# Down projection by seven products: weight sums prepared on GpSimd among the z products, low parts of two units in one operation

## The reference

```python
def layer(x, pos, lp, cache):
    a_u, a_v, b_q, b_k, b_v, c_q, c_k, c_v, c_o, c_logi, c_logf = project(
        x, pos, lp['attn_norm'], lp['w_in'], lp['gmlp_norm'], lp['mlstm_gate_b'])
...
    x = x + mixed @ lp['w_out']
    y, conv_state = conv_ffn(x, lp['ffn_norm'], lp['w_up'], lp['conv_w'], lp['conv_b'], lp['w_down'], conv_buf)
    x = x + y
...

def conv_ffn(x, g, w_up, conv_w, conv_b, w_down, conv_buf):
    up = rmsnorm(x, g) @ w_up
    T = up.shape[1]
    full = jnp.concatenate([conv_buf.astype(up.dtype), up], axis=1)
    c = conv_b + full[:, 0:T] * conv_w[0]
    for j in range(1, CONV_W):
        c = c + full[:, j:j + T] * conv_w[j]
    y = (jax.nn.gelu(c[..., :D_FF], approximate=False) * c[..., D_FF:]) @ w_down
    return y, full[:, -(CONV_W - 1):]
```

## Time and profile before

| | |
|---|---|
| runs (us) | 2410.37, 2413.76, 2416.2; median 2413.76 |
| profiled execution | 2414.81 us, of which the span of the trace is 2413.0 us |
| mean granted TensorE clock | 0.995 |
| busy: TensorE / VectorE / ScalarE / GpSimd | 98% / 70% / 46% / 31% of the span |
| DMA | 264.83 MB, mean 110 GB/s |

### The profile page before, as it was taken

One profiled execution on the slowest core, in us unless ns is written; L12 is line 12 of the kernel. 1 busy time (PEld: TensorE's weight loads), 2 busy tenths in 40 slices (PEclk: granted clock), 3 DMA queues, 4 the chain that ended last, 5 costly groups with the idle time before them and its releaser, 6 DMA issues.

```text
span 2413.0 us, 42532 instructions
## 1 busy us (share of the span) xinstructions
PE 2360.4 (98%) x16563; PEld 2315.0 (96%) x16563; DVE 1682.6 (70%) x2875; ACT 1116.8 (46%) x2227; POOL 742.7 (31%) x732
## 2 busy tenths in 40 slices
PE   9999999999999999999999999999999999998999
PEld 8999998999999998999999999999999999998999
DVE  3115687888788877888611256877987888779884
ACT  6325676544433433345523366655333333333563
POOL 0001254432222223664110013452322222245630
PEclk9999999999999999999999999999999999999999
DMA  4442432212221224454524334321222222253564
GB/s 155 135 142 89 147 114 53 73 64 81 72 80 64 81 72 150 161 165 137 196 73 139 120 125 136 100 60 54 81 78 74 72 73 75 86 214 93 161 198 148
DMA packets 248348, 264.83 MB, mean 110 GB/s; under 512 B 16822, under 2 KB 212564, under 8 KB 245972
## 3 DMA queue, kind: packets, MB, share of 16 engines
q1 hardware_dynamic: 248148, 262.11, 34.3%
HBM read 211.95 MB, written 50.11 MB: 109 GB/s over the span
## 4 chain that ended last, share of the span: by engine, by line
PE 78%; DVE 12%; issue 4%; POOL 2%; ACT 2%; DMA 2%; SPq 0%; DVEq 0%; POOLq 0%; ACTq 0%
PE bank L401 24%; PE bank L403 23%; PE bank L402 23%; DVE sA L2729 3%; DVE sB L2731 3%; PE bank L1367 1%; PE bank L1292 1%; PE bank L1337 1%; DMA grr<-g_scratch 1%; DVE xT L2740 1%; DVE tb L2726 1%; PE bank L1377 1%; POOL wN L2187 1%; POOL acc L453 1%; DVE sD L2731 1%
## 5 line engine op out<-in xcount | busy, mean ns | idle before, releaser
L401 PE MATMUL bank<-actH,wb 128*128 128x384 f32 (+1 forms) x1712 | 560.8, 328 | 1.5 <-DVE actL L2607 1.3
L402 PE MATMUL bank<-actL,wb 128*128 128x384 f32 (+1 forms) x1712 | 555.5, 324 | 0.0
L403 PE MATMUL bank<-actH,wb 128*128 128x384 f32 (+1 forms) x1712 | 555.1, 324 | 0.0
L401 PE MATMUL bank<-wzH,actH 128*128 128x256 f32 (+3 forms) x1296 | 369.4, 285 | 2.8 <-issue 1.5
L403 PE MATMUL bank<-wzH,actL 128*128 128x256 f32 (+3 forms) x1296 | 364.2, 281 | 0.0
L402 PE MATMUL bank<-wzL,actH 128*128 128x256 f32 (+3 forms) x1296 | 363.9, 281 | 0.0
L401 PEld LDWEIGHTS bank<-actH,wb 128*128 128x128 f32 x1712 | 322.8, 189 | 6.2 <-issue 3.2
L402 PEld LDWEIGHTS bank<-actL,wb 128*128 128x128 f32 x1712 | 323.7, 189 | 0.7
L403 PEld LDWEIGHTS bank<-actH,wb 128*128 128x128 f32 x1712 | 323.7, 189 | 0.0
L401 PEld LDWEIGHTS bank<-wzH,actH 128*128 128x128 f32 (+1 forms) x1296 | 236.3, 182 | 4.9 <-issue 2.0
L402 PEld LDWEIGHTS bank<-wzL,actH 128*128 128x128 f32 (+1 forms) x1296 | 236.5, 182 | 0.0
(11 more groups left out here) (361 smaller groups left out, 5526.6 us busy)
## 6 DMA issues: line engine op xcount, KB each, us to landing
raw<-in_w_up SPq DMA_DIRECT2D x88, 512.0 KB, 4.5
g_scratch<-cv SPq DMA_DIRECT2D x44, 545.0 KB, 3.1
rawz<-in_w_in SPq DMA_DIRECT2D x22, 1024.0 KB, 5.4
zb<-z_scratch SPq DMA_DIRECT2D x16, 1156.0 KB, 6.1
z_scratch<-zst SPq DMA_DIRECT2D x128, 128.0 KB, 1.8
raw<-in_w_out SPq DMA_DIRECT2D x128, 128.0 KB, 2.9
grr<-g_scratch SPq DMA_DIRECT2D x38, 384.0 KB, 3.3
raw<-in_w_down SPq DMA_DIRECT2D x50, 256.0 KB, 3.4
```

What stands on the lines that cost most here:

```text
L401: pe.matmul(out, aH, bH, start=first, stop=False, skip_group_check=goes_on)
L402: pe.matmul(out, aH, bL, start=False, stop=False, skip_group_check=goes_on)
L403: return pe.matmul(out, aL, bH, start=False, stop=last, skip_group_check=goes_on)
```

## The change

Weight sums. A DRAM scratch `ws_scratch` takes the four weight sums of each j. They are made among the z products: SyncE loads both row blocks of pair i (1 MB, `load_parts`) into one of two places of `stg` behind the store of unit 9 + 3i, GpSimd makes four sums of 512 columns (`weight_parts`), and SyncE stores them (1 MB, `store_sums`) behind the store of unit 13 + 3i, ahead of `next_wz` and `load_mixers` at the same u. `load_parts(i)` waits for the store of pair i − 2. `stg` lies where `zb0` lies, so `load_zb(0)` waits for the last two stores. GpSimd makes the sums of pairs 0 to 5 ahead of its `memset`s and those of 6 to 10 behind them.

Down products. `w_down` is no longer kept; `load_w` brings for each step the two weight operands, raw or summed. High parts (`step_high`) and low parts (`step_parts`) are made for both halves in one operation (1024 and 768 wide) for p < 3; p = 3 keeps 512 and 384. All gate sums, T2 among them, are GpSimd's (`gate_sum`, 44 per layer). The parts of steps 0 to 4 are made among the taps of the last up products; before, those of the first seven units. There are four operand slots, by t mod 4; gates stay in `pbA` and `pbB`. Both adds of product pair p − 1 follow step j = 1 of p. The `convst` transposes move behind unit (3, 1, 2) into bank 2, ScalarE's copy to p = 3, j = 6, the store behind the ninth load of the last chunk. The loads of the last chunk wait for later steps (`load_half(j)` for j < 4: steps 40 and 41; before: the first unit of p = 3).

```diff
+        ws_dram = nc.dram_tensor("ws_scratch", (DEPTH, NJ, P, 4, 512), F32, kind="Internal").ap()
...
+        def w_slot(t):
+            return sA0 if t % 4 == 0 else sA3 if t % 4 == 3 else sA1[:, t % 4 - 1]
+        def g_slot(t):
+            return sB3 if t % 4 == 3 else sB[:, t % 4]
+        def g_pair(j):
+            return pbA[:, j] if j < 6 else pbB[:, j - 6]
+        def w_parts(t):
+            if t < 3 * NJ:
+                return w_raw(t)[:, 0:2], w_slot(t)[:, 0:2, 0], w_slot(t)[:, 0:2, 1]
+            return w_raw(t)[:, 1], w_slot(t)[:, 1, 0], w_slot(t)[:, 1, 1]
+        def g_parts(t):
+            p, j = t // NJ, t % NJ
             if p == 3:
+                return g_pair(j)[:, 1], sD[:, j % 4, 0], sD[:, j % 4, 1]
+            src = grr[:, j % 3, 1:3] if p == 2 else g_pair(j)[:, 0:2]
+            return src, g_slot(t)[:, 0:2, 0], g_slot(t)[:, 0:2, 1]
...
+        def step_low(l, t):
+            return l * N_W + 2 * NF + 2 * t + 2
+        def slot_free(l, t):
+            if t < 4:
+                return tile_mm(l, NF - 1, (2, 6, 9, 9)[t])
+            p, j = (t - 4) // NJ, (t - 4) % NJ
+            if t >= 3 * NJ:
+                return unit_mm(l, p, 1, j)
+            return max(unit_mm(l, p, h, j) for h in range(2))
...
+                    elif i == 0:
+                        sp.wait_ge(ws_st[0], ws_stored(l, NJ - 1))
+                        sp.wait_ge(ws_st[1], ws_stored(l, NJ - 2))
...
+                def load_parts(i):
+                    if i >= 2:
+                        sp.wait_ge(ws_st[i % 2], ws_stored(l, i - 2))
+                    sp.dma_start(stg[:, i % 2, 0:4].rearrange("p (k h) n -> p k (h n)", k=2),
+                                 w_down[2 * i * P:2 * i * P + 2 * P, :].rearrange("(k p) n -> p k n", p=P)).then_inc(ws_in[i % 2], 16)
+                def store_sums(i):
+                    sp.wait_ge(s_r, w_sum_at(l, i, 3))
+                    sp.dma_start(ws_dram[l, i], stg[:, i % 2, 1:5]).then_inc(ws_st[i % 2], 16)
                 for u in range(Z1):
                     store_z(u)
+                    if u >= 9 and u % 3 == 0 and u // 3 - 3 < NJ:
+                        load_parts(u // 3 - 3)
+                    if u >= 13 and u % 3 == 1 and u // 3 - 4 < NJ:
+                        store_sums(u // 3 - 4)
                     if u == 5:
                         next_wz(2)
...
+                    if t >= 4:
+                        sp.wait_ge(w_l, step_low(l, t - 4))
+                    place, r0, r1 = w_raw(t), slice(2 * j * P, 2 * j * P + P), slice(2 * j * P + P, 2 * j * P + 2 * P)
                     if p == 0:
-                        sp.dma_start(w_raw(f), w_down[f * P:f * P + P, :]).then_inc(ld_in[t % 3], 16)
-                    c = slice(0, 512) if p == 1 else slice(512, 1024)
-                    sp.dma_start(w_raw(f + 1)[:, c], w_down[f * P + P:f * P + 2 * P, c]).then_inc(ld_in[t % 3], 16)
+                        sp.dma_start(place[:, 0], ws_dram[l, j, :, 3]).then_inc(ld_in[t % 3], 16)
+                        sp.dma_start(place[:, 1], w_down[r0, 0:512]).then_inc(ld_in[t % 3], 16)
+                    elif p == 1:
+                        sp.dma_start(place[:, 0:2], ws_dram[l, j, :, 1:3]).then_inc(ld_in[t % 3], 16)
+                    elif p == 2:
+                        sp.dma_start(place[:, 0], w_down[r1, 0:512]).then_inc(ld_in[t % 3], 16)
+                        sp.dma_start(place[:, 1], ws_dram[l, j, :, 0]).then_inc(ld_in[t % 3], 16)
+                    else:
+                        sp.dma_start(place[:, 1], w_down[r1, 512:1024]).then_inc(ld_in[t % 3], 16)
...
+                    if p in (1, 3):
+                        sp.wait_ge(w_l, step_low(l, t - NJ if p == 1 else t - 2 * NJ))
+                    elif p == 2 and j >= 3:
+                        sp.wait_ge(w_l, step_low(l, t - 3))
+                    pair = g_pair(j)
+                    if p == 0:
+                        sp.dma_start(pair.rearrange("p c t -> p (c t)"), g_dram[l, 2 * j, :, 0:768]).then_inc(ld_in[t % 3], 16)
+                    elif p == 1:
+                        sp.dma_start(pair[:, 1], g_dram[l, 2 * j + 1, :, 0:384]).then_inc(ld_in[t % 3], 16)
+                    elif p == 2:
+                        sp.dma_start(grr[:, j % 3, 0:2].rearrange("p c t -> p (c t)"), g_dram[l, 2 * j + 1, :, 0:768]).then_inc(ld_in[t % 3], 16)
+                        sp.dma_start(grr[:, j % 3, 2], g_dram[l, 2 * j, :, 0:384]).then_inc(ld_in[t % 3], 16)
+                    else:
+                        sp.dma_start(pair[:, 1], g_dram[l, 2 * j + 1, :, 384:768]).then_inc(ld_in[t % 3], 16)
...
+                load_w(2)
                 for t in range(3):
                     load_gs(t)
-                load_gs(3)
-                for t in range(2, 5):
+                for t in range(3, 4 * NJ):
                     load_w(t)
-                for t in range(4, 4 * NJ):
                     load_gs(t)
-                    if t + 1 < 3 * NJ:
-                        load_w(t + 1)
-                    if t == 7:
+                    if t == 9:
                         store_g(NF - 1)
-                    if t == 8:
-                        sp.wait_ge(gv_st, l * 16 + 16)
-                        sp.wait_ge(sto_r, 2 * l + 2)
-                        for s, dst in ((0, "prompt_conv"), (1, "sample_conv")):
-                            sp.dma_start(O[dst][l, 0].rearrange("r (a b) -> (r a) b", b=P), cvo[:, s]).then_inc(cvo_st, 16)
+                def store_conv():
+                    sp.wait_ge(gv_st, l * 16 + 16)
+                    sp.wait_ge(sto_r, 2 * l + 2)
+                    for s, dst in ((0, "prompt_conv"), (1, "sample_conv")):
+                        sp.dma_start(O[dst][l, 0].rearrange("r (a b) -> (r a) b", b=P), cvo[:, s]).then_inc(cvo_st, 16)
 
                 def load_half(j):
                     h, f, q = j // NF, j % NF, j % 4
                     if j < 4:
-                        sp.wait_ge(w_l, unit_low(l, 3, 1, 0))
+                        sp.wait_ge(w_l, step_low(l, 4 * NJ - 4 + j // 2))
...
+                        if j == 8:
+                            store_conv()
...
-                    if (p, h, j) == (0, 0, 0):
+                    if (p, h, j) == (3, 1, 2):
                         pe.wait_ge(cvs_r, (l + 1) * 4 * NF)
+                        pe.wait_ge(bank_free, product_out(l, 2, 0, 2))
                         for s in range(2):
-                            q = pe.transpose(bank[7][0:88, s * P:(s + 1) * P],
+                            q = pe.transpose(bank[2][0:88, s * P:(s + 1) * P],
...
+                            if m == 2:
+                                pe.wait_ge(sto_r, 2 * l + 2)
...
+                def step_high(t):
+                    raw_w, w_hi, _ = w_parts(t)
+                    raw_g, g_hi, _ = g_parts(t)
+                    act.wait_ge(mm, slot_free(l, t))
+                    act.wait_ge(ld_in[t % 3], ld_at(l, t))
+                    act.activation(w_hi, raw_w, ACT.Copy).then_inc(w_h, 1)
+                    act.wait_ge(s_r, g_sum_at(l, t))
+                    act.activation(g_hi, raw_g, ACT.Copy).then_inc(w_h, 1)
...
-                for p, h, j in UNITS[5:]:
-                    unit_high(p, h, j)
-                    if (p, h) == (2, 0) and 4 <= j < 8:
+                for t in range(4, 4 * NJ):
+                    step_high(t)
+                    p, j = t // NJ, t % NJ
+                    if p == 2 and 4 <= j < 8:
                         norm_square(act, n, 0, j - 4, x_added(l, 0, j - 4))
                     if p == 3 and 3 <= j < 7:
                         norm_square(act, n, 0, j + 1, x_added(l, 0, j + 1))
+                    if p == 3 and j == 6:
+                        act.wait_ge(stt_r, 2 * l + 2)
+                        act.wait_ge(gv_st, l * 16 + 16)
+                        act.activation(cvo, bank[2][0:88, 0:256].rearrange("p (s t) -> p s t", s=2), ACT.Copy).then_inc(sto_r, 1)
...
-                    act.wait_ge(mm, half_mm(l, j - 8) if j >= 8 else unit_mm(l, 3, 1, 1 if j < 4 else NJ - 1))
+                    act.wait_ge(mm, half_mm(l, j - 8) if j >= 8 else unit_mm(l, 3, 1, (7, 7, 9, 10)[min(j, 3)]))
...
+                def weight_parts(i):
+                    A11, A21, A12, A22, S1 = (stg[:, i % 2, k] for k in range(5))
+                    pool.wait_ge(ws_in[i % 2], ws_loaded(l, i))
+                    pool.tensor_tensor(S1, A21, A22, ALU.add).then_inc(s_r, 1)
+                    pool.tensor_tensor(A21, A11, A21, ALU.subtract).then_inc(s_r, 1)
+                    pool.wait_ge(s_r, w_sum_at(l, i, 0))
+                    pool.tensor_tensor(A22, S1, A11, ALU.subtract).then_inc(s_r, 1)
+                    pool.wait_ge(s_r, w_sum_at(l, i, 2))
+                    pool.tensor_tensor(A12, A12, A22, ALU.subtract).then_inc(s_r, 1)
+                for i in range(6):
+                    weight_parts(i)
...
+                for i in range(6, NJ):
+                    weight_parts(i)
...
+                def gate_sum(t):
```

(32 more changed lines are left out.)

248 lines of the change are left out of this document (64 added, 184 removed).

## The result

The changed kernel takes 2420.85 us (median of 18 runs, 2416.98 to 2423.24), the kernel before beside it 2414.15 us: ratio 1.0026, interval 1.0019 to 1.0033. It is slower by a quarter of a per cent. (One of the 18 runs of the kernel before took 7302.56 us and has no part in the ratio.) The forecast was 2414 us and "no change" as the likeliest single outcome, with a range of 2380 to 2436 us. Behind the small difference stand two large ones: the down products gave 46 us, the z products took 52 us.

The account below looks back on a forecast made before the run. The prediction took TensorE to be the bound, its down products held up by VectorE, which GpSimd slows. From 2414.8 us it took 32 us of gain and added 31 us of cost among the z products: 2414 us, range 2380 to 2436 us.

Parts of the forecast that it names:

- the DMA share from 55 to 160 us: Sign among the z products that the forecast is right: a share over 0.85, with TensorE waiting near units 32 and 45.
- Gain 32 us (bounds 15 and 38): Down products, both layers: fewer, wider VectorE operations and fewer GpSimd sums there remove waits and lower-clock time.
- together 39.9. Left 2 × 4 = 8: Down products: 30.6 us of waits plus 9.3 us of lower clock are removable; 4 us per layer stay.
- the reserve of 3 us at the start of a stage: Down products: 3 us per layer left because steps 0 and 1 need double-width parts from both engines.
- that of 1 us in the last seventh: Down products' last seventh: 1 us per layer left, as one-unit steps with two sets of adds have no slack.
- Slows VectorE half as long: Down products: GpSimd's sums fall from 89 us to 44 us per layer, so it slows VectorE half as long.
- Fewer and wider operations: Down products: VectorE's 165 operations per layer become 88, alone 85 us instead of 100 us.
- Cost 31 us (bounds 3 and 50): z products, both layers: 14 us of waits plus 1.4 us of lower clock per layer from the sums' transfers.
- the cycle of a slot: z products: load, sums and store take 18.5 to 20.1 us against 16.9; 2 us lost per cycle, 7 us in all.
- the load of group 8 and the late load 3: z products: load 3 starts 5.5 us late, and group 8's load stands 2 us longer behind other transfers.
- The second rival, the queue as the bound of the z products: z products: queue full at 357 GB/s, 25 us per layer lost, 2433 us; chance 0.17.
- The first, the queue that keeps up: z products: transfers run at 410 GB/s, only group 8 is late, 2386 us; chance 0.27.
- The third, late loads in the down products: Down products: landings past 9.1 us lose half the gain, 2431 us; chance 0.10.

Follow-up runs that it names:

- run 8: Kernel before the change, with GpSimd summing 16 of 512 columns in S1, S2 and S3 of the down products: 2377.78 us, ratio 0.9848.
- run 9: Changed kernel with VectorE's low parts and gates split in two again for the 33 steps of two units: 2421.10 us, ratio 1.0034.
- run 10: Changed kernel with three operand slots instead of four, parts of steps 3 and 4 made after the last up products: 2441.54 us, ratio 1.0114.
- run 7: As run 6, but S3 made in the third pass of the down products again, three sums stored instead of four: 2374.49 us, ratio 0.9847.
- run 2: Changed kernel with GpSimd summing only 16 of 512 columns from the third pair on, transfers and order kept: 2423.56 us, ratio 1.0042.
- run 4: Changed kernel with three `stg` slots (sums in place), weight loads issued ahead of the sums' transfers, stores one unit later: 2392.90 us, ratio 0.9913.
- run 6: As run 4, but transfers start at unit 4, at most one per unit; seven pairs summed ahead of the `memset`s: 2383.61 us, ratio 0.9873.
- run 5: As run 4 with three slots, but everything issued where the changed kernel issues it: 2410.56 us, ratio 0.9990.

## Why the prediction was right or wrong

**The direction of both halves, and the places: right.** TensorE's waits for `xT`, `sB`, `vn` and `sD` went, the clock there is 1.00, and TensorE waits for `wzL` and `zst` instead (23.5 and 16.9 us), because SyncE stands in order and its transfers land late. That gain and loss nearly cancel was forecast. That the time came within 7 us of the forecast is luck all the same: both terms lie outside their bounds, the gain by 14 us from its value and the cost by 21, and the two errors cancel. Of the signs it named, the DMA share from 55 to 160 us was to be over 0.85 and is 0.81, because the queue had gaps.

**"Gain 32 us (bounds 15 and 38)": too small, 46 us.** The step that failed is "together 39.9. Left 2 × 4 = 8". Nothing was left: the reserve of 3 us at the start of a stage measured 1.0 us of waits for `upb`, that of 1 us in the last seventh 0.0. The waits were sized right: the two stretches of the earlier trace rows have 185.00 − 171.01 + 186.40 − 169.91 = 30.5 us in which TensorE is not busy. The other 15.8 us are busy time, 171.01 and 169.91 us to 162.57 in either layer, where the sum has 9.3 us for the clock. The clock is not the term that was too small. In the stages of the kernel before it was at its lower level in three stretches:

```profile
998.57:1005.40 6.83, 6.00 (x19) 6.03 (x20) 6.83 (x15) 3.02 (x6) 2.05 (x2) 0.50 0.28 74
1053.19:1056.60 3.41, 3.41 (x13) 3.41 (x12) 3.41 (x7) 0.55 (x2) 1.28 (x2) 0.50 0.10 12
2138.62:2145.45 6.83, 5.82 (x18) 5.82 (x19) 6.83 (x5) 5.53 (x12) 6.83 (x5) 0.50 0.72 289
```

These are 17.1 us at half speed, which can cost 8.5 us at most; by the starts of consecutive matmuls they cost some 7. The term that the sum lacks altogether is what a wait costs beyond its idle time, some 9 us by the same starts: the matmul in flight ahead of a wait counts as busy for 0.34 us where in a full stream the next one starts after 0.174 us (30 waits, 5 us), and some 50 delays are too short to show as idle time at all (some 4 us more than after).

**Why the gain came: half right.** "Slows VectorE half as long" is the larger part (run 8: 16.0 of 22.4 and 17.7 of 23.8 us). "Fewer and wider operations" was the heading of the part, and its width is worth nothing in the changed kernel (run 9), although the estimate of 0.95 us for 768 wide came out as 0.948. The fourth slot (run 10), which had one clause, is worth some 11 us per layer. The two overlap: in run 8 three slots were enough for 169 us. By the Trainium skill, GPSIMD Engine Reference, Key points, GpSimd shares its memory interfaces with VectorE instructions that have two inputs there; run 8 agrees, with 29.3 us of VectorE for 36.6 us of GpSimd. That moving T2 over would by itself cost was not tried; in the changed kernel the stage has room for it, and in run 7 for 11 larger sums too.

**"Cost 31 us (bounds 3 and 50)": too small, 52 us, just outside its bounds.** Waits: 20.2 us per layer (23.5 + 16.9 in both) instead of 14; of the other 26 − 20.2 = some 6 us, 5 are matmuls at the lower clock, by the starts of consecutive matmuls, instead of 1.4. The step that failed is the cycle of a slot, "a load (5.4 us as `rawz`), 5.4 us of sums, and a store" of 4.6 us: shorter sums changed nothing (run 2), and the store took 7.5 us in the median over the execution (4.0 us at the least, so the 4.6 us were right for a quiet queue). Its landing, against two units from `store_sums(i)` to `load_parts(i + 2)`, 5.6 us, is what SyncE stood for, some 2 us eight times (16.4 us). So SyncE fell back by some 2 us, as forecast, but at each load, which is twice in a cycle of six units: 16.4 us where the sum has 7. Too kind was also the reading that only the load of group 8 and the late load 3 come on top: all six weight loads from 73 to 161 us landed late, after 7.1 to 9.7 us instead of 5.4.

**The second rival, the queue as the bound of the z products (2433 us, 0.17)**, has the right number for that half, its 50 us is 2 from what was measured, but only part of the mechanism. The queue was not full: its share was 0.81 at 281 GB/s, and run 4 moved the same volume with a lag 30 us smaller over both layers. The forecast's own mechanism, SyncE's order and its waits, is the larger part; of the 22 us that run 4 leaves, runs 6 and 7 take another 12, by spreading the transfers and by less volume. The first, the queue that keeps up, has the trace against it: 5.7 us for the loads of `stg` and 7.5 us for the stores, in a queue that is shared. (The Trainium skill, DMA: Bandwidth & Descriptors, Anatomy of one DMA, gives an estimated 4.4 us for either on GpSimd's issuing path; on SyncE's shared queue the trace does not agree.) The third, late loads in the down products, did not occur (no wait there).

## What to carry to other kernels

Work moved to an idle engine is free only if its transfers are: cost them on the queue that they share, in order, with every wait that the issuing engine takes for them, and put the loads that the critical engine waits for first (7 us here). A ring of buffers has to cover the landing under load (here 7.5 us for 1 MB, not the 4.6 us worked out from the quiet kernel), and when one wait is taken from an engine that issues in order, the next takes its place, so try order and depth together (7 and 10 us alone, 28 us together with a later store, by the medians). Where one engine's work slows another, as GpSimd's sums slowed VectorE, take work away from the first (16.0 and 17.7 us) before making the second one's operations wider (nothing).

## What was not expected of the hardware

How long a transfer of 1 MB took to land went with what else was in the queue more than with its kind. In the changed kernel the stores of the sums took 7.5 us in the median and the loads of `stg` 5.7; with three slots and the other order (run 4) it was 7.1 and 7.3 us, with three slots alone (run 5) 6.0 and 6.2. Single stores of the changed kernel landed after 4.0 to 10.1 us. One queue with z stores, weight loads and sums gave 320 GB/s at a share of 0.90 (run 4), and 357 GB/s in a full stretch of the kernel before; the "410 GB/s and more" that the prediction read from the single 545 KB store was no guide to it. And 20 us of waits cost some 5 us per layer in clock: with the wait of 11.34 us in it the stretch from 160 to 186 us had a mean granted clock of 0.74.
